# Two transformer blocks on one core: the order of the PSUM banks in the down products, other banks for one rotary slab, and a norm taken in two halves of the tokens

## The chip, the core and the metric

The kernel runs on one core of a Trainium2 chip. The metric is the device time of one execution in microseconds; times of a kernel are given as the median of several runs. One more execution, taken by the hardware profiler, is the one whose rows are shown here. TensorE (PE) multiplies and writes to PSUM, which has eight banks of 128 x 512 float32; VectorE (DVE), ScalarE (ACT) and SyncE's DMA queue do the rest. The granted clock is the clock of TensorE that the profile records, 1.0 for 2.4 GHz and 0.5 for 1.2 GHz.

## The reference

Two different blocks run one after the other over x of 512 tokens by 1024 features, all in float32. The first has attention (4 heads) beside a gated linear recurrence, a gated MLP with 2816 hidden features and a gated projection of a second input. The second has retention and a spatial gating branch, a normed output projection, and an MLP with a convolution over the tokens:

```
h = rms_norm(x, g_ffn); x = x + (silu(h @ w_gate) * (h @ w_up)) @ w_down          # first block
q, k, v, g, u, sv, a_ret, a_sgu = split(rms_norm(x, g_pre_mix_2) @ w_in_2)          # second block
merged = sigmoid(a_ret) * retention(rotary(q), rotary(k), v, g) + sigmoid(a_sgu) * sgu(u, sv)
x = x + rms_norm(merged @ w_out_2, g_post_mix_2)
h2 = rms_norm(x, g_pre_ffn_2)
x = x + rms_norm(conv_gated_mlp(h2, w_up_2, conv_w_2, conv_b_2, w_down_2), g_post_ffn_2)
```

## The kernel before

**Slabs.** The weights come as 130 slabs of at most 128 x 2048, in the order of the list `slabs`, through a ring of three buffers. SyncE loads a slab as soon as TensorE has finished the one three before it. For each slab ScalarE writes `slab_hi`, a float32r copy (L1873, `split`), and VectorE writes `slab_lo`, the rest (L1067, `split`). Activations are split in the same way into `h_hi` and `h_lo`. A product is then three matmuls, hi by hi, hi by lo and lo by hi (`three`, L380 to L382), and so nearly all matmuls of the kernel carry these three lines.

**Order.** Each engine's program is a Python function (`tensor_program`, `vector_program`, `scalar_program`, `sync_program`), written out by hand in the order in which the engine runs it. Engines wait for each other by semaphores. TensorE's results go into the eight PSUM banks: `take(name, b)` makes TensorE wait until the reader of what bank b held before is done, and `whole` tells the readers that a tile is complete. `slab_fm` multiplies one slab of 256 output features into two tiles of 128 features by 512 tokens; without another choice slab g takes the banks 2*(g%2) and 2*(g%2)+1. `rot` hands out the banks 4 to 7 in turn for small tiles.

**The down products of the first block** (`down`). Eight tiles of 128 features by 512 tokens, one in each bank, are summed over 11 slabs. All eight banks are taken ahead of the first matmul. The slab before (the last `up` slab) has its tiles in banks 0 and 1; VectorE reads them at L1490.

**The second block's down products** (`down_tokens`) are the same with the tokens on the partitions: block t of 128 tokens has its two halves of the features in banks 2t and 2t+1. All eight banks are again taken first. The last `b2up` tiles are in banks 0 and 1, read at L1109.

**The rotary slabs.** The second block starts with four slabs for queries and keys. Slabs IN2 and IN2+1 run together and fill four tiles in banks 2, 3, 0, 1; slabs IN2+2 and IN2+3 take banks 2, 3 and 0, 1 again. Of each tile ScalarE copies the two halves (L2210, L2211) and VectorE multiplies the tile itself out of its bank (L1567).

**The norm behind w_out.** Four slabs give eight tiles `o2`. ScalarE squares each (L2329, into `tmp[k]`) and copies it with its gain (L2330), VectorE sums the squares into `tmp[0]` (L1080), TensorE sums over the features with matmuls of one column (L441), ScalarE takes the root (L1878), VectorE the reciprocal (L1091) and lays it on a diagonal (L1094, `diagonal`), and TensorE multiplies ones by it (L990), which gives the row `post_row` of 512 tokens on all partitions. For each tile k VectorE multiplies `o2` by the row (L1785) and adds it to the residual `xT` (L1790); ScalarE writes `h_hi` (L2347) and a square for the next norm (L2348), and VectorE `h_lo` (L1072). Then the first two `up` slabs of the convolution MLP, UP2 and UP2+1, run together, tile k of the features after tile k, over four banks. Behind them VectorE sums the squares and splits slab UP2+2.

**The attention part.** In the loop over n (8 passes) ScalarE copies the transposed softmax weights of unit u out of PSUM (`transposed`, L2007), which TensorE's value products wait for (L694), and from n = 5 on rounds a gated head to `gated_hi` (`head_output`, L2063), which VectorE needs for `gated_lo`. From n = 6 on `transposed` has nothing left to do there.

## Time and profile before

| | us |
|---|---|
| median of 3 runs | 1635.32 |
| lowest, highest | 1631.61, 1635.99 |
| the profiled execution, its whole time | 1637.03 |
| its span | 1635.7 |
| TensorE busy in it | 1610.8 |
| VectorE, ScalarE busy in it | 885.4, 650.7 |
| mean granted clock | 0.994 |

The span is the time from the first to the last record of the profiled execution. TensorE's matmuls overlap: a matmul of 512 columns is recorded as 0.39 us long while the next one starts 0.23 us after it. In the chain of waits each piece therefore counts from one end to the next. The granted clock is 1.0 for the whole span except for three stretches, near 82 to 93 us, near 1257 to 1267 us and at the very end.

### The profile page before, as it was taken

Reading aid. Unit: us, or ns where it says so; the run is one execution under the profiler, and the core shown is the slowest. Engines: PE = TensorE matmul, PEld = TensorE weight load, DVE = VectorE, ACT = ScalarE, POOL = GpSimd, SP = SyncE. Lnnn points to the kernel's source line nnn. Section 1 sums busy time; section 2 is a strip of 40 time slices with the busy share of each in tenths; the row PEclk is TensorE's granted clock in tenths of the full one; section 3 lists DMA queues with packets and bytes.
Section 4 is the critical chain, followed back from the end, with each engine's and each line's share of the span. In section 5 each row is a group of like instructions: output and inputs, shape, how many; then the busy total and the mean of one; then the engine's idle time right before and its main releaser. Section 6 shows DMA issues by size and latency. Waiting matters only on the chain.

```text
span 1635.7 us, 17948 instructions
## 1 busy us (share of the span) xinstructions
PE 1610.8 (98%) x7508; PEld 1318.6 (81%) x7508; DVE 885.4 (54%) x1178; ACT 650.7 (40%) x783; POOL 11.7 (1%) x25
## 2 busy tenths in 40 slices
PE   7999999999999999999999999999998999999998
PEld 6787777888888888888798888888886888888887
DVE  5646656774444441257655644354444787766313
ACT  4536657543232221155443433223334453444212
POOL 1000000000000000000000000000000000000000
PEclk9989999999999999999999999999998999999999
DMA  5311110213333323323221133222323232232232
GB/s 166 97 52 58 46 52 27 71 59 116 103 103 103 96 86 103 103 97 103 89 99 52 56 105 103 82 89 88 103 77 103 78 104 82 99 103 92 101 103 78
DMA packets 117216, 144.25 MB, mean 88 GB/s; under 512 B 6017, under 2 KB 103648, under 8 KB 117136
## 3 DMA queue, kind: packets, MB, share of 16 engines
q1 hardware_dynamic: 115712, 139.88, 26.1%
q0 software_dynamic: 1232, 3.16, 0.6%
q8 instruction: 60, 0.98, 0.3%
q14 instruction: 20, 0.16, 0.0%
q10 hardware_dynamic: 192, 0.07, 0.0%
HBM read 140.99 MB, written 2.10 MB: 87 GB/s over the span
## 4 chain that ended last, share of the span: by engine, by line
PE 95%; ACT 2%; DVE 2%; DMA 1%; issue 0%; SPq 0%; POOL 0%; DVEq 0%; ACTq 0%
PE bank L380 28%; PE bank L382 28%; PE bank L381 28%; PE bank L913 1%; PE bank L676 1%; PE bank L694 1%; PE bank L675 1%; PE bank L739 1%; PE bank L896 1%; PE bank L615 1%; PE bank L441 1%; ACT slab_hi L1873 1%; PE bank L734 1%; DMA slab_raw<-in_w_in 0%; PE bank L685 0%
## 5 line engine op out<-in xcount | busy, mean ns | idle before, releaser
L380 PE MATMUL bank<-h_hi,slab_hi 128*128 128x512 f32 x1192 | 473.9, 398 | 5.2 <-DVE h_lo L1072 3.1
L1067 DVE TENSOR_TENSOR slab_lo<-slab_raw,slab_hi 128x2048 fp32r<-128x2048 f32 x130 | 296.1, 2278 | 334.3 <-ACT slab_hi L1873 333.7
L382 PE MATMUL bank<-h_hi,slab_lo 128*128 128x512 f32 x1192 | 466.1, 391 | 0.0
L381 PE MATMUL bank<-h_lo,slab_hi 128*128 128x512 f32 x1192 | 465.8, 391 | 0.0
L1873 ACT ACTIVATE slab_hi<-slab_raw 128x2048 fp32r<-128x2048 f32 x130 | 246.5, 1897 | 175.1 <-DMA slab_raw<-in_w_down 142.6
L380 PEld LDWEIGHTS bank<-h_hi,slab_hi 128*128 128x128 f32 x1192 | 224.8, 189 | 58.4 <-issue 10.3
L381 PEld LDWEIGHTS bank<-h_lo,slab_hi 128*128 128x128 f32 x1192 | 225.0, 189 | 47.9 <-issue 2.2
L382 PEld LDWEIGHTS bank<-h_hi,slab_lo 128*128 128x128 f32 x1192 | 224.8, 189 | 47.5
L1109 DVE TENSOR_TENSOR tmp<-bank,x_rstd_rows 128x512 f32<-128x512 f32 x98 | 66.6, 687 | 95.7 <-PE bank L382 95.6
L380 PE MATMUL bank<-slab_hi,h_hi 128*128 128x256 f32 (+1 forms) x224 | 74.8, 334 | 0.0
L382 PE MATMUL bank<-slab_hi,h_lo 128*128 128x256 f32 (+1 forms) x224 | 73.6, 328 | 0.0
L381 PE MATMUL bank<-slab_lo,h_hi 128*128 128x256 f32 (+1 forms) x224 | 73.5, 328 | 0.0
L380 PE MATMUL bank<-slab_hi,hid_hi 128*128 128x512 f32 x176 | 68.6, 389 | 0.8 <-issue 0.8
L380 PE MATMUL bank<-hid_hi,slab_hi 128*128 128x512 f32 x176 | 68.5, 389 | 0.8 <-issue 0.8
L381 PE MATMUL bank<-slab_lo,hid_hi 128*128 128x512 f32 x176 | 68.5, 389 | 0.0
L382 PE MATMUL bank<-hid_hi,slab_lo 128*128 128x512 f32 x176 | 68.5, 389 | 0.0
L381 PE MATMUL bank<-hid_lo,slab_hi 128*128 128x512 f32 x176 | 68.5, 389 | 0.0
L382 PE MATMUL bank<-slab_hi,hid_lo 128*128 128x512 f32 x176 | 68.5, 389 | 0.0
L2366 ACT ACTIVATE tmp<-tmp,param_cols 128x512 f32<-128x512 f32 x44 | 35.2, 814 | 76.8 <-DVE tmp L1109 76.7
L380 PE MATMUL bank<-y_hi,slab_hi 128*128 128x512 f32 x128 | 50.3, 393 | 0.0
L382 PE MATMUL bank<-y_hi,slab_lo 128*128 128x512 f32 x128 | 49.8, 389 | 0.0
L381 PE MATMUL bank<-y_lo,slab_hi 128*128 128x512 f32 x128 | 49.8, 389 | 0.0
(417 smaller groups left out, 2142.7 us busy)
## 6 DMA issues: line engine op xcount, KB each, us to landing
slab_raw<-in_w_in SPq DMA_DIRECT2D x40, 1024.0 KB, 5.0
slab_raw<-in_w_up SPq DMA_DIRECT2D x33, 1024.0 KB, 5.0
slab_raw<-in_w_down SPq DMA_DIRECT2D x22, 1024.0 KB, 4.9
slab_raw<-in_w_gate SPq DMA_DIRECT2D x11, 1024.0 KB, 5.2
slab_raw<-in_w_o SPq DMA_DIRECT2D x4, 1024.0 KB, 4.9
slab_raw<-in_w_ple_gate SPq DMA_DIRECT2D x4, 1024.0 KB, 5.0
slab_raw<-in_w_ret_o SPq DMA_DIRECT2D x4, 1024.0 KB, 4.9
slab_raw<-in_w_sgu_o SPq DMA_DIRECT2D x4, 1024.0 KB, 4.9
```

Of the source, the lines that this page charges most:

```text
L380: T.matmul(ps, a_hi, b_hi, start=start, stop=False, skip_group_check=skip)
L381: T.matmul(ps, a_hi, b_lo, start=False, stop=False, skip_group_check=skip)
L382: return T.matmul(ps, a_lo, b_hi, start=False, stop=stop, skip_group_check=skip)
L441: ins = T.matmul(dst[:, t:t + 1], sq[:, chunk[t]], ones[:, 0:1], start=clear and t == 0, stop=last, skip_group_check=True)
L615: ins = T.matmul(sums[:, c:c + which.shape[1]], tmp[n % 4][:, chunk[t]], which, start=n == 0 and t == 0, stop=n >= 5, skip_group_check=True)
L675: T.matmul(ps[:, :], q_nope[:, hd, chunk[j]], k_nope[:, hd, :], start=True, stop=False)
L676: whole(("score", u), T.matmul(ps[:, :], q_rope[half, hd // 2, chunk[j]], k_rope[half, hd // 2, :], start=False, stop=True))
L694: ins = T.matmul(ps[:, :], v_mla[:, kb, hd * VH:(hd + 1) * VH], p_t[:, kb, :], start=kb == 0, stop=kb == TT - 1)
L1067: V.tensor_tensor(w_lo[j][:, 0:n], raw[j][:, 0:n], w_hi[j][:, 0:n].bitcast(F32), ALU.subtract).then_inc(slab_lo, 1)
L1109: V.tensor_tensor(dst, t.ps[:, :], xrow[:, :], ALU.mult).then_inc(t.free, 1)
L1873: A.activation(w_hi[j][:, 0:n], raw[j][:, 0:n], ACT.Copy).then_inc(slab_hi, 1)
L2366: A.activation(acc[t], hid[t], ACT.Identity, scale=col("conv_w1", f[t]), bias=col("conv_b_2", f[t])).then_inc(conv_mid, 1)
```

## The change

**The down products.** `down` takes each bank only when its first product is due, in slab 0, and goes through slab 0 in another order of the banks: 4, 5, 6, 7, then the two that the slab before last had, then the two of the last slab. `down_tokens` does the same by blocks of tokens: 2, 3, 1, 0. The other slabs keep their order.

**The rotary slab.** IN2+2 takes banks 4 and 5. IN2+3 keeps 0 and 1.

**The norm behind w_out.** VectorE's last addition of squares is left out; TensorE sums tile 0 (the sum of seven) and tile 7 into the same column of a bank. The diagonal, the row product (banks 7 and 5), and for tile 0 the product, the addition and `h_hi` go by halves of 256 tokens. In the first two `up` slabs TensorE takes, for each k, the products of `h_hi` first (eight matmuls, for k = 0 sixteen of half the width) and waits for `h_lo` only then (four matmuls). For the tiles behind tile 0 VectorE's product is also two instructions, one from each bank.

**ScalarE's order.** `head_output` stands behind `transposed`.

```diff
-        def slab_fm(g, names, src_hi=h_hi, src_lo=h_lo, ready=None, src=None):
+        def slab_fm(g, names, src_hi=h_hi, src_lo=h_lo, ready=None, src=None, b=None):
...
-            ps = [take(names[t], 2 * (g % 2) + t) for t in range(2)]
+            ps = [take(names[t], (2 * (g % 2) if b is None else b) + t) for t in range(2)]
...
         def down(g0, name, hi, lo, lo_done):
-            ps = [take((name, n), n) for n in range(KT)]
+            last = 2 * ((g0 - 1) % 2)
+            order = [4, 5, 6, 7, 2 - last, 3 - last, last, last + 1]
...
-                for n in range(KT):
+                for n in order if s == 0 else range(KT):
+                    ps = tile[name, n].ps if s else take((name, n), n)
...
-        for n in range(2, 4):
-            slab_fm(IN2 + n, [("rot", 2 * n), ("rot", 2 * n + 1)])
+        slab_fm(IN2 + 2, [("rot", 4), ("rot", 5)], b=4)
+        slab_fm(IN2 + 3, [("rot", 6), ("rot", 7)])
...
-        whole("post_sum", sum_rows(ps[:, 0:TT], tmp[0], True, True))
-        T.wait_ge(post_diag, 1)
-        ps = take("post_row", 7, post_done, KT)
-        whole("post_row", T.matmul(ps[:, :], ones, tmp[1], start=True, stop=True))
+        sum_rows(ps[:, 0:TT], tmp[0], False, True)
+        T.wait_ge(post_squared, KT)
+        whole("post_sum", sum_rows(ps[:, 0:TT], tmp[KT - 1], True, False))
+        for half in range(2):
+            T.wait_ge(post_diag, half + 1)
+            ps = take(("post_row", half), 7 - 2 * half, post_done, KT)
+            whole(("post_row", half), T.matmul(ps[:, 0:CW], ones, tmp[1][:, half * CW:(half + 1) * CW], start=True, stop=True))
...
         for k in range(KT):
-            for s in range(2):
-                part(wv, s, names, *h_k, k, k + 1, h_ready(5))
+            for half in range(2 if k == 0 else 1):
+                tok = slice(half * CW, (half + 1) * CW) if k == 0 else slice(0, S)
+                if k == 0 and half == 0:
+                    T.wait_ge(first_hi_half, 1)
+                else:
+                    T.wait_ge(h_hi_done, 8 * 5 + k + 1)
+                for n in range(4):
+                    hv, lv = wv[n // 2]
+                    cols_t, ps = slice((n % 2) * P, (n % 2 + 1) * P), tile[names[n]].ps
+                    T.matmul(ps[:, tok], hv[:, k, cols_t], h_hi[:, k, tok], start=k == 0 and half == 0, stop=False,
+                             skip_group_check=True)
+                    T.matmul(ps[:, tok], lv[:, k, cols_t], h_hi[:, k, tok], start=False, stop=False, skip_group_check=True)
+            T.wait_ge(h_lo_done, 8 * 5 + k + 1)
+            for n in range(4):
+                hv, cols_t = wv[n // 2][0], slice((n % 2) * P, (n % 2 + 1) * P)
+                ins = T.matmul(tile[names[n]].ps[:, :], hv[:, k, cols_t], h_lo[:, k, :], start=False, stop=k == KT - 1,
+                               skip_group_check=True)
...
-        ps = [take(("down2", n), n) for n in range(2 * TT)]
+        last = (DOWN2 - 1) % 2
+        blocks_first = [2, 3, 1 - last, last]
...
+                ps = take(("down2", 2 * t + half), 2 * t + half) if f == 0 else tile["down2", 2 * t + half].ps
...
-            for t in range(TT):
+            for t in range(TT) if s else blocks_first:
```

On VectorE and ScalarE:

```diff
-        sum_tiles(tmp, post_squared, 0, 5, KT - 1)
+        sum_tiles(tmp, post_squared, 0, 5, KT - 1, post_summed)
         split(UP2 + 1)
-        sum_tiles(tmp, post_squared, 0, KT - 1, KT, post_summed)
         rstd(rcol[:, 0:TT], "post_sum")
-        diagonal(tmp[1], rcol[:, 0:TT], post_diag)
...
+        for half in range(2):
+            t, tok = tile["post_row", half], slice(half * CW, (half + 1) * CW)
+            V.wait_ge(psum_ready, t.done)
+            V.wait_ge(vector_step, step(V.tensor_tensor(tmp[2][:, tok], o2[:, 0, tok], t.ps[:, 0:CW], ALU.mult)))
+            V.tensor_tensor(xT[:, 0, tok], xT[:, 0, tok], tmp[2][:, tok], ALU.add).then_inc((post_half, post_done)[half], 1)
...
+        A.wait_ge(post_half, 1)
+        A.activation(h_hi[:, 0, 0:CW], xT[:, 0, 0:CW], ACT.Identity, scale=col("g_pre_ffn_2", 0)).then_inc(first_hi_half, 1)
         for k in range(KT):
             A.wait_ge(post_done, k + 1)
-            A.activation(h_hi[:, k, :], xT[:, k, :], ACT.Identity, scale=col("g_pre_ffn_2", k)).then_inc(h_hi_done, 1)
+            tok = slice(0 if k else CW, S)
+            A.activation(h_hi[:, k, tok], xT[:, k, tok], ACT.Identity, scale=col("g_pre_ffn_2", k)).then_inc(h_hi_done, 1)
```

TensorE at the start of the first down products, before. The last row of the `up` slab (source `h_hi`) stands first; the names behind the arrow are what streams and what is loaded as weights, with the number of the buffer.

```order
L382 MATMUL bank1<-h_hi_66,slab_lo1_61 128x512
L380 MATMUL bank0<-hid_hi_117,slab_hi2_65 128x512
L381 MATMUL bank0<-hid_lo_118,slab_hi2_65 128x512
L382 MATMUL bank0<-hid_hi_117,slab_lo2_62 128x512
L380 MATMUL bank0<-hid_hi_117,slab_hi2_65 128x512
```

And now (line numbers here and below are those of the changed kernel):

```order
L383 MATMUL bank1<-h_hi_66,slab_lo1_61 128x512
L381 MATMUL bank4<-hid_hi_117,slab_hi2_65 128x512
L382 MATMUL bank4<-hid_lo_118,slab_hi2_65 128x512
L383 MATMUL bank4<-hid_hi_117,slab_lo2_62 128x512
L381 MATMUL bank4<-hid_hi_117,slab_hi2_65 128x512
```

The product behind the last `up` tile (bank 1) goes to bank 4 instead of bank 0, and bank 1 comes last, 42 matmuls later.

TensorE at the norm behind w_out, before: the last product of w_out, the sum over features, the row, and the first products of UP2 and UP2+1.

```order
L382 MATMUL bank1<-merged_hi_144,slab_lo0_60 128x512
L441 MATMUL bank6<-const_small_sb_77,tmp0_69 128x1 x4
L990 MATMUL bank7<-tmp1_70,const_small_sb_77 128x512
L380 MATMUL bank2<-h_hi_66,slab_hi1_64 128x512
L381 MATMUL bank2<-h_lo_67,slab_hi1_64 128x512
L382 MATMUL bank2<-h_hi_66,slab_lo1_61 128x512
```

And now:

```order
L383 MATMUL bank1<-merged_hi_144,slab_lo0_60 128x512
L442 MATMUL bank6<-const_small_sb_77,tmp0_69 128x1 x4
L442 MATMUL bank6<-const_small_sb_77,tmp7_76 128x1 x4
L997 MATMUL bank7<-tmp1_70,const_small_sb_77 128x256
L997 MATMUL bank5<-tmp1_70,const_small_sb_77 128x256
L1019 MATMUL bank2<-h_hi_66,slab_hi1_64 128x256
L1021 MATMUL bank2<-h_hi_66,slab_lo1_61 128x256
```

There are two sums and two half rows, and the first product of `h_lo` has moved from the second to the seventeenth matmul of the slab pair.

VectorE at the same place, before:

```order
L1080 TENSOR_TENSOR tmp_69<-tmp_69,tmp_76 128x512
L1091 RECIPROCAL rstd_cols<-rstd_cols 128x4
L1094 TENSOR_TENSOR tmp_70<-const_small_sb,rstd_cols 128x512
L1785 TENSOR_TENSOR tmp_71<-mixed_out,bank 128x512
L1790 TENSOR_TENSOR residual<-residual,tmp_71 128x512
L1785 TENSOR_TENSOR tmp_72<-mixed_out,bank 128x512
L1072 SCALAR_TENSOR_TENSOR h_lo<-residual,param_cols,h_hi 128x512
L1790 TENSOR_TENSOR residual<-residual,tmp_72 128x512
```

And now:

```order
L1118 RECIPROCAL rstd_cols<-rstd_cols 128x4
L1804 TENSOR_TENSOR tmp_70<-const_small_sb,rstd_cols 128x256 x2
L1811 TENSOR_TENSOR tmp_71<-mixed_out,bank 128x256
L1812 TENSOR_TENSOR residual<-residual,tmp_71 128x256
L1811 TENSOR_TENSOR tmp_71<-mixed_out,bank 128x256
L1812 TENSOR_TENSOR residual<-residual,tmp_71 128x256
L1821 TENSOR_TENSOR tmp_72<-mixed_out,bank 128x256 x2
L1099 SCALAR_TENSOR_TENSOR h_lo<-residual,param_cols,h_hi 128x512
L1827 TENSOR_TENSOR residual<-residual,tmp_72 128x512
```

The addition of squares (L1080) is gone, the diagonal and the work on tile 0 stand in halves, and two halves stand for each later product.

## Rows read from the trace of the kernel before

**Rows 1.** The page: busy us of each engine, share of the span, instructions.

```profile
PE 1610.8 (98%) x7508; PEld 1318.6 (81%) x7508; DVE 885.4 (54%) x1178; ACT 650.7 (40%) x783; POOL 11.7 (1%) x25
```

**Rows 2.** The chain of waits at the first down products: start us, us, what.

```profile
591.60 0.83 issue
592.43 0.47 PE bank L380
592.90 0.23 PE bank L381
```

**Rows 3.** The timeline of VectorE there: start us, us, engine, line, operation, [idle before].

```profile
591.64 0.69 DVE L1490 TENSOR_TENSOR tmp<-tmp,bank 128x512 f32<-128x512 f32 x1 [2.60 <-PE bank L382]
```

**Rows 4.** The timeline of TensorE at the second block's down products.

```profile
1510.66 0.47 PE L380 MATMUL bank<-slab_hi,hid_hi 128*128 128x512 f32 x1 [0.83 <-issue]
```

**Rows 5.** The chain of waits ahead of the third rotary slab.

```profile
792.26 0.61 DVE ret_qk L1567
...
793.01 0.47 PE bank L380
```

**Rows 6.** The timeline of TensorE ahead of the third rotary slab.

```profile
791.87 0.39 PE L382 MATMUL bank<-h_hi,slab_lo 128*128 128x512 f32 x1
```

**Rows 7.** The chain of waits in the attention part.

```profile
281.85 0.52 ACT gated_hi L2063
282.37 0.49 ACT weights_t L2007
282.90 3.70 PE bank L694 x8
```

**Rows 8.** The chain of waits at the norm behind w_out.

```profile
1253.33 0.61 ACT tmp L2329
...
1253.96 0.70 DVE tmp L1080
...
1254.71 1.07 PE bank L441 x8
...
1256.31 0.70 DVE tmp L1094
...
1257.05 2.09 PE bank L990 x2
...
1259.16 0.70 DVE tmp L1785
...
1260.61 0.73 ACT h_hi L2347
...
1261.37 0.76 DVE h_lo L1072
...
1262.27 0.76 PE bank L380
```

**Rows 9.** Groups by line: engine, operation, xcount | busy us, mean ns | idle.

```profile
L1626 DVE COPY ret_state_b<-bank 128x256 f32<-128x256 f32 x4 | 1.7, 424 | 0.1
...
L1897 ACT ACTIVATE ret_v<-bank,x_rstd_cols 128x256 f32<-128x256 f32 x4 | 1.9, 474 | 17.7 <-PE bank L382 17.7
```

**Rows 10.** The timeline of TensorE among products of 256 columns.

```profile
843.01 0.28 PE L380 MATMUL bank<-slab_hi,h_hi 128*128 128x256 f32 x1
843.13 0.28 PE L381 MATMUL bank<-slab_lo,h_hi 128*128 128x256 f32 x1
```

**Rows 11.** The timeline of VectorE, slab UP2+2.

```profile
1282.01 2.29 DVE L1067 TENSOR_TENSOR slab_lo<-slab_raw,slab_hi 128x2048 fp32r<-128x2048 f32 x1
```

**Rows 12.** The timeline of TensorE, its first matmul on slab UP2+2.

```profile
1287.12 0.49 PE L380 MATMUL bank<-h_hi,slab_hi 128*128 128x512 f32 x1
```

**Rows 13.** Stretches: us, busy time by engine, PEclk (granted clock), DMA share, GB/s.

```profile
1256.00:1257.00 1.00, 0.00 (x0) 0.00 (x0) 0.87 (x2) 0.06 (x1) 0.00 (x0) 0.82 1.08 385
...
1266.00:1267.00 1.00, 1.00 (x5) 0.77 (x3) 1.00 (x3) 0.14 (x1) 0.00 (x0) 0.56 0.00 0
```

**Rows 14.** A stretch in the first block's query projection, same columns.

```profile
82.50:83.50 1.00, 1.00 (x4) 0.81 (x3) 0.00 (x0) 0.00 (x0) 0.00 (x0) 0.50 0.00 0
```

More of the change, by code:

```diff
@@ L1769, in vector_program @@
         split(UP2)
[L1770 removed]
+        sum_tiles(tmp, post_squared, 0, 5, KT - 1, post_summed)
         split(UP2 + 1)
[L1774 removed]
         rstd(rcol[:, 0:TT], "post_sum")
[L1776 to L1779 removed]
+        for half in range(2):
+            two = slice(2 * half, 2 * half + 2)
+            V.tensor_tensor(per_tile(tmp[1])[:, two, :], ident.unsqueeze(1).broadcast_to([P, 2, P]),
+                            rcol[:, two].unsqueeze(2).broadcast_to([P, 2, P]), ALU.mult).then_inc(post_diag, 1)
+        emptied(("o2", 0))
+        for half in range(2):
+            t, tok = tile["post_row", half], slice(half * CW, (half + 1) * CW)
+            V.wait_ge(psum_ready, t.done)
+            V.wait_ge(vector_step, step(V.tensor_tensor(tmp[2][:, tok], o2[:, 0, tok], t.ps[:, 0:CW], ALU.mult)))
+            V.tensor_tensor(xT[:, 0, tok], xT[:, 0, tok], tmp[2][:, tok], ALU.add).then_inc((post_half, post_done)[half], 1)
+        for k in range(1, KT + 1):
             if k < KT:
@@ L1784, in vector_program @@
                 emptied(("o2", k))
-                scaled_step = step(V.tensor_tensor(w, o2[:, k, :], t.ps[:, :], ALU.mult))
-            if k:
-                norm_tile(5, k - 1, "g_pre_ffn_2")
+                for half in range(2):
+                    tok = slice(half * CW, (half + 1) * CW)
+                    scaled_step = step(V.tensor_tensor(w[:, tok], o2[:, k, tok], tile["post_row", half].ps[:, 0:CW], ALU.mult))
+            if k == 1:
+                V.wait_ge(first_hi_half, 1)
+            norm_tile(5, k - 1, "g_pre_ffn_2")
             if k < KT:
@@ L2104, in scalar_program @@
             transposed(unit)
+            if n >= 5:
+                head_output(n - 5)
             unit += 1
```

12 lines of the change are left out of this document (5 added, 7 removed).

## The prediction, made before the changed kernel was run

> **What bounds the kernel now.** I read the page's busy times first, then the chain of waits, then the timeline at the places that the diff touches. TensorE is busy for 98% of the span [rows 1], so an edit can only pay where TensorE stands still or runs at the lower clock, and any VectorE or ScalarE time elsewhere is free as long as it stays hidden. The steady spacing of two 512-column matmuls is 0.23 us [rows 2]. Against that spacing the chain shows five holes at edited places: one ahead of the first block's down products, one ahead of the third rotary slab, one inside the attention part, one ahead of the second block's down products, and a large one at the norm behind w_out.
>
> **The banks of the down products.** Before the first matmul all eight banks are asked for. The last one to come free is that of the last `up` tile, which VectorE reads from 591.64 for 0.69 us [rows 3]. TensorE's hole is 0.83 us, and the first matmul behind it takes 0.47 us where 0.23 is the rule [rows 2], so 0.83 + 0.24 = 1.07 us. After the change bank 4 is asked for alone, and the late bank stands last of eight: seven banks at six matmuls of 0.23 us is 9.6 us of cover, against 0.7 us of need. The hole goes, **-1.07 us**. Nothing else takes its place: the slab and the `hid_lo` tiles of slab 0 were made long before. The second down products show the same 0.83 and 0.47 us [rows 4]; the last `b2up` tiles stand in banks 0 and 1, and token block 0 now goes last in slab 0, again with over 8 us of cover: **-1.07 us**.
>
> **The rotary slab.** Its tiles 4 and 5 take banks 2 and 3 from tiles 0 and 1. VectorE's read of tile 1 ends at 792.87 and TensorE starts at 793.01 [rows 5]; its last matmul had begun at 791.87 [rows 6], so the steady start would be 792.10. The second matmul of the restart ends 1.0 us later than in a steady stream (793.48 is the end of the first, 792.49 would be): **-1.0 us**. Banks 4 and 5 were last used for the norm's sum and row, read by then. What is late next? Tiles 6 and 7 stay in banks 0 and 1, where tiles 2 and 3 are read several us before; the value tiles that want banks 4 and 5 come a whole slab later, 48 matmuls or 10.9 us.
>
> **ScalarE's order in the attention part.** For n = 5 alone both operations exist. The copy `weights_t` starts at 282.37, right behind `gated_hi` with its 0.52 us, and TensorE starts at 282.90 when it is whole [rows 7]. With the copy first it is whole 0.52 us earlier: **-0.5 us**. `gated_hi` and its reader on VectorE come 0.5 us later; the states that TensorE needs next are then due some 2 us before their use.
>
> **The norm behind w_out.** The old path runs from 1253.33 to 1262.27, 8.9 us [rows 8]. The new one, step by step:
> 1. Square of tile 7, 0.63 as before.
> 2. VectorE's last addition, 0.70 us, is gone from the path. Instead TensorE sums two tiles. The first sum needs nothing late and runs beside the square; one group costs 1.07 us [rows 8], so it ends near 1254.1 to 1254.3, and the second at about 1255.1, where the old one ended at 1255.78. Gain about 0.7 (0.5 if the groups don't overlap at all).
> 3. Root and reciprocal, 0.53 us, unchanged.
> 4. Half a diagonal. No 128x256 TENSOR_TENSOR stands in the trace; a COPY of that size takes 0.42 us, a scaled copy on ScalarE 0.47 [rows 9], against 0.70 for the whole. I take 0.42 + 0.04.
> 5. Half the row product: 1.04 of 2.09 us, as before at the lower clock.
> 6. Half a product and half an addition on VectorE, 0.44 each for 0.72 each.
> 7. `h_hi` by half, 0.49 for 0.75.
> 8. `h_lo`, 0.76 us, is no longer waited for, since the first eight matmuls read h_hi alone. The 0.14 us to issue stay.
> The sum is 1.77 + 0.53 + 0.46 + 1.06 + 0.88 + 0.49 + 0.14 = 5.3 us, so TensorE starts near 1258.65: **-3.6 us**. Then 16 matmuls of 256 columns stand for 8 of 512; their spacing is 0.12 us [rows 10], so +0.1 us. The second half of h_hi is due 0.9 us behind the first, h_lo 0.9 us after that; eight matmuls of 256 columns take 1.0 us at the full clock and 1.7 at half, so TensorE hardly waits.
>
> What is late next is VectorE. It splits slab UP2+2 behind the norm: that ends at 1284.30 [rows 11], and TensorE wants it at 1287.12 [rows 12], 2.8 us of slack. TensorE comes 3.6 us earlier. VectorE's products begin 2.0 us earlier, but it pays 0.3 us more for tile 0 and up to 0.15 us (0.42 twice for 0.70) for each of seven others. So the split ends 0.6 to 1.7 us earlier, at 1282.6 to 1283.7, and is wanted at 1283.5: between 0.9 us of slack and 0.2 us of wait. I take no wait.
>
> **The clock.** It fell at about 1256.6 (0.82 over that microsecond) and rose at 1266.9 (0.56) [rows 13], so TensorE ran its first 4.6 us of matmuls at 1.2 GHz, which costs 2.3 us. The new path still leaves TensorE with little to do for over 3 us (two groups of one-column sums, then a pause, then a short product, then a pause), so I take the same loss again, with 0.8 us either way for where the rise falls. The row at 82.5 us, at 0.50 [rows 14], shows that short pauses among thin matmuls can lower it too.
>
> **The sum.** 1.07 + 1.07 + 1.0 + 0.5 + 3.6 - 0.1 = 7.2 us. The profiled execution took 1637.03 us (span 1635.7 and 1.3 around it), which gives 1629.8. The median of the runs shown lies 0.1% below it, at 1635.32; the same ratio gives **1628.1 us**, 0.44% faster.
>
> **Rivals.**
> A, the forecast: 1628.1, by itself 1626.5 to 1630. Chance 0.62.
> B, the clock stays up or rises early at the norm. The pauses are now 1 to 1.5 us each, where the longest was 3.1. That gives back up to 2.3 us and 0.5 us of the row product: 1625.3. For it: shorter pauses. Against: [rows 14]. Chance 0.12. The Trainium skill ("TensorE: Matmul & The Clock Gate", HAM oscillation) blames long idle gaps alone; by that B would be the likelier, and the trace at 82.5 us speaks against it.
> C, the norm gives half. VectorE's halves cost nearly a whole operation each, 0.6 for 0.70: four steps on the path then save 0.1 instead of 0.26, so the path is 0.6 us longer, tile 0 costs VectorE 1.0 us more than before and each of the seven later pairs some 0.5. The split of slab UP2+2 then ends at 1284.3 - 1.4 + 1.0 + 3.5 = 1287.4 and is wanted at 1284.1. That gives back 0.6 + 3.3 = 3.9 us: 1632.0. The point from which it decides is 0.45 us for a half. Against it are the sizes in [rows 9]. Chance 0.16. The Trainium skill ("VectorE: DVE Perf Modes", the TRN2 errata) advises tiles of 512 elements or more because each instruction pays a fixed part; by that rule the halves are a mistake, and here what counts is the time to the first half, not VectorE's total.
> D, the edits at the down products do nothing, because the bank that is asked for first is also late. Against: banks 4 to 7 hold transposes read long before. Both terms fall out: 1630.2. Chance 0.06.
> E, slower. In the first slab of both down products eight waits now stand one by one between matmuls. If each, though satisfied, stops the preloading of weights, 14 added stops are paid. A stop with a real wait costs 1.0 us [rows 5, 6]; at that price the kernel is 14 - 7.2 = 7 us slower, 1642. It decides from 0.51 us a stop. Against: slabs begin all over the trace with three waits and no hole. Chance 0.04.
>
> **Numbers.** The bound of 0.3% (4.9 us, about what a measurement of this kernel can tell from no change) lies at 1630.4. Most of C, half of D and a twentieth of A lie above it. So faster 0.76, same 0.20, slower 0.04. The range reaches from B less the clock's 0.8 us to C, and the runs before span 4 us by themselves: 1624.5 to 1632.5.
>
> **What would show it.** In the profile after: no hole ahead of either down product, nor ahead of the third rotary slab; `weights_t` ahead of `gated_hi`; TensorE's first h_hi matmul 5.3 us behind the square of tile 7, the diagonal halves at 0.42 us; a low stretch of 4 to 5 us behind it; no idle TensorE ahead of slab UP2+2. A hole of 1 us or more there, or waits between the banks of slab 0, would make the prediction wrong.

## The result and the profile after

| | before | after |
|---|---|---|
| median, us | 1635.13 (4 runs) | 1625.53 (4 runs, 1624.66 to 1628.76) |
| ratio | | 0.995, interval 0.9935 to 0.9965 |
| the profiled execution | 1637.03 | 1628.76 |
| its span | 1635.7 | 1627.5 |
| TensorE busy | 1610.8 | 1608.6 |

The forecast was 1628.1 us within 1624.5 to 1632.5. The medians differ by 9.6 us where 7.2 were predicted; the profiled executions differ by 8.2 us of span. Ratios leave out slow executions: one of the kernel before, drawn beside `late_sum`, `best_a` and `best_b` below, took 5535 us.

The page of the changed kernel gives the busy time of each engine, as in [rows 1]. Line numbers are from here on those of the kernel that is spoken of; in the changed one `three` is L381 to L383.

```profile
PE 1608.6 (99%) x7526; PEld 1319.1 (81%) x7526; DVE 885.4 (54%) x1187; ACT 651.0 (40%) x784; POOL 11.7 (1%) x25
```

But for 18 matmuls more at the norm, both traces run the same ones in nearly the same order. So one can take the start of a matmul before, less its start after, and see where this difference, called the offset from here on, grows. That is the whole account of the 8.2 us:

| place | a matmul before, after | gained there |
|---|---|---|
| up to 100 us, code that the change doesn't touch | 100.19, 98.62 | 1.57 |
| ScalarE's order, attention part | 282.90, 280.80 | 0.53 |
| first down products | 593.66, 590.46 | 1.10 |
| third rotary slab | 794.02, 789.79 | 1.03 |
| norm behind w_out | 1286.31, 1278.48 | 3.60 |
| second down products, their start | 1512.13, 1503.19 | 1.11 |
| second down products, second slab | 1521.87, 1513.60 | -0.67 |

The changed places give 6.7 us. Of the 1.57 us in the first row, 0.14 stand already at 60 us and 1.43 arise in the query projection near 82 us, where nothing was changed.

**First down products.** TensorE's timeline, against [rows 2]: start us, us, engine, line, operation. The first product of `hid_hi` follows 0.23 us behind the last `up` matmul.

```profile
589.10 0.39 PE L383 MATMUL bank<-h_hi,slab_lo 128*128 128x512 f32 x1
589.33 0.39 PE L381 MATMUL bank<-hid_hi,slab_hi 128*128 128x512 f32 x1
```

VectorE's read of the last `up` tile, against [rows 3], now lies beside TensorE's products, and its bank is wanted 9.6 us later:

```profile
589.53 0.69 DVE L1517 TENSOR_TENSOR tmp<-tmp,bank 128x512 f32<-128x512 f32 x1 [2.60 <-PE bank L383]
```

**Third rotary slab**, TensorE's timeline, against [rows 5, 6]: no hole.

```profile
788.66 0.39 PE L383 MATMUL bank<-h_hi,slab_lo 128*128 128x512 f32 x1
788.89 0.39 PE L381 MATMUL bank<-h_hi,slab_hi 128*128 128x512 f32 x1
```

**Attention part**, ScalarE's timeline, against [rows 7]: the copy that TensorE wants now stands first.

```profile
280.17 0.58 ACT L2044 ACTIVATE weights_t<-bank 128x512 f32<-128x512 f32 x1
280.65 0.62 ACT L2100 ACTIVATE gated_hi<-z 128x512 fp32r<-128x512 f32 x1
```

**The norm behind w_out**, the chain of waits (start us, us, what), against [rows 8]. The x16 row is both sums over features; from it to the last row is the new path.

```profile
1249.05 1.75 PE bank L442 x16
...
1250.83 0.27 ACT rstd_cols L1915
...
1251.34 0.44 DVE tmp L1804
...
1251.82 0.71 PE bank L997 x2
...
1252.62 0.43 DVE tmp L1811
...
1253.08 0.44 DVE residual L1812
...
1253.54 0.52 ACT h_hi L2383
1254.06 0.14 issue
1254.19 0.55 PE bank L1019
```

**Second down products.** TensorE no longer stands ahead of their first slab, but ahead of their second. Its timeline there, with the idle time and its releaser in brackets:

```profile
1512.49 0.39 PE L383 MATMUL bank<-slab_hi,hid_lo 128*128 128x512 f32 x1
1513.26 0.50 PE L381 MATMUL bank<-slab_hi,hid_hi 128*128 128x512 f32 x1 [0.39 <-DVE slab_lo L1094]
1513.60 0.39 PE L382 MATMUL bank<-slab_lo,hid_hi 128*128 128x512 f32 x1
```

What it waits for, on ScalarE and VectorE:

```profile
1507.58 1.28 ACT L2415 ACT_TABLE_LOAD   x1
1508.87 0.20 ACT L2415 ACTIVATE rstd_cols<-const_small_sb 128x1 f32<-128x1 f32 x1
1508.98 3.70 ACT L1910 ACTIVATE slab_hi<-slab_raw 128x2048 fp32r<-128x2048 f32 x2
```

```profile
1510.91 4.50 DVE L1094 TENSOR_TENSOR slab_lo<-slab_raw,slab_hi 128x2048 fp32r<-128x2048 f32 x2 [2.63 <-ACT slab_hi L1910]
```

ScalarE finishes `hid_hi` of the last tiles, loads its table for the square root (1.28 us) and only then splits the next slab; VectorE's first `slab_lo` of the pair is whole 2.3 us later, at 1513.2, where steady products would want it at 1512.7. In the kernel before, the same piece stood here, VectorE's timeline and then TensorE's:

```profile
1518.75 4.49 DVE L1067 TENSOR_TENSOR slab_lo<-slab_raw,slab_hi 128x2048 fp32r<-128x2048 f32 x2 [2.63 <-ACT slab_hi L1873]
```

```profile
1521.65 0.39 PE L380 MATMUL bank<-slab_hi,hid_hi 128*128 128x512 f32 x1
```

It was whole at 1521.0 and wanted at 1521.65: 0.6 us of slack. Taking 1.07 us away upstream spent it. The Trainium skill ("ScalarE: Activation LUTs", What ACT_TABLE_LOAD costs) gives 1.28 us for the load and some 1.38 us of drain beside it. The trace agrees on the load; the next operation starts 0.01 us behind it and the load itself 0.02 us behind `hid_hi`, so no such drain shows here.

**Slab UP2+2**, VectorE's split and TensorE's first matmul on it, against [rows 11, 12]:

```profile
1275.60 2.28 DVE L1094 TENSOR_TENSOR slab_lo<-slab_raw,slab_hi 128x2048 fp32r<-128x2048 f32 x1
```

```profile
1279.29 0.49 PE L381 MATMUL bank<-h_hi,slab_hi 128*128 128x512 f32 x1
```

Whole at 1277.9, used at 1279.3: 1.4 us of slack are left of 2.8, and no wait.

**The clock.** Stretches of 12 us over the two places where it falls: us, busy time by engine, granted clock, DMA share, GB/s. One less the granted clock, times 24, is the length of the stretch at 1.2 GHz. Before:

```profile
82.00:94.00 12.00, 12.00 (x45) 10.37 (x44) 2.61 (x5) 2.06 (x4) 0.00 (x0) 0.57 0.01 1
1256.00:1268.00 12.00, 7.81 (x18) 5.08 (x19) 8.90 (x15) 4.75 (x9) 0.00 (x0) 0.57 0.15 52
```

After:

```profile
82.00:94.00 12.00, 12.00 (x57) 10.41 (x56) 2.96 (x5) 3.63 (x4) 0.00 (x0) 0.73 0.09 17
1252.00:1264.00 12.00, 11.12 (x45) 9.20 (x45) 10.89 (x24) 6.50 (x11) 0.00 (x0) 0.72 0.12 42
```

At 82 us it is 10.2 us at the lower clock before and 6.8 us after (the latter began at 81.7). At the norm it is 10.2 and 6.8 us too, but of these only what has matmuls in it costs: 4.6 us before, 5.1 us after (1254.19 to 1259.3). The norm's gain is thus 3.84 us at the first product and 3.60 us at the end. The fall comes 3.5 us behind the last product of w_out in both traces; what differs is how long the clock stays low.

### The profile page after: what moved, and what is told of

Read it like the earlier page. It is cut to its first block, busy times and chain, and to the rows that moved or that the text cites. A ratio compares the mean times of both kernels' runs of the same rounds, so it can differ in the third digit from the quotient of the medians.

```text
span 1627.5 us, 17987 instructions
## 1 busy us (share of the span) xinstructions
PE 1608.6 (99%) x7526; PEld 1319.1 (81%) x7526; DVE 885.4 (54%) x1187; ACT 651.0 (40%) x784; POOL 11.7 (1%) x25
## 4 chain that ended last, share of the span: by engine, by line
PE 95%; DVE 2%; ACT 1%; DMA 1%; issue 0%; SPq 0%; POOL 0%; DVEq 0%; ACTq 0%
PE bank L381 28%; PE bank L383 28%; PE bank L382 28%; PE bank L917 1%; PE bank L677 1%; PE bank L695 1%; PE bank L676 1%; PE bank L740 1%; PE bank L900 1%; PE bank L442 1%; ACT slab_hi L1910 1%; DVE slab_lo L1094 1%; PE bank L616 1%; DMA slab_raw<-in_w_in 1%; PE bank L1019 1%; PE bank L735 1%
## 5 line engine op out<-in xcount | busy, mean ns | idle before, releaser
L381 PE MATMUL bank<-h_hi,slab_hi 128*128 128x512 f32 x1160 | 460.1, 397 | 1.6 <-DVE h_lo L1156 1.3
L383 PE MATMUL bank<-h_hi,slab_lo 128*128 128x512 f32 x1160 | 452.7, 390 | 0.0
L382 PE MATMUL bank<-h_lo,slab_hi 128*128 128x512 f32 x1160 | 452.2, 390 | 0.0
L381 PEld LDWEIGHTS bank<-h_hi,slab_hi 128*128 128x128 f32 x1160 | 218.3, 188 | 51.2 <-issue 4.4
L382 PEld LDWEIGHTS bank<-h_lo,slab_hi 128*128 128x128 f32 x1160 | 218.3, 188 | 46.7 <-issue 2.2
L383 PEld LDWEIGHTS bank<-h_hi,slab_lo 128*128 128x128 f32 x1160 | 218.1, 188 | 46.1
L381 PE MATMUL bank<-slab_hi,h_hi 128*128 128x256 f32 (+1 forms) x224 | 74.8, 334 | 0.0
L383 PE MATMUL bank<-slab_hi,h_lo 128*128 128x256 f32 (+1 forms) x224 | 73.6, 328 | 0.0
L381 PE MATMUL bank<-slab_hi,hid_hi 128*128 128x512 f32 x176 | 68.6, 390 | 0.4 <-DVE slab_lo L1094 0.4
L383 PE MATMUL bank<-slab_hi,hid_lo 128*128 128x512 f32 x176 | 68.5, 389 | 0.0
L381 PE MATMUL bank<-hid_hi,slab_hi 128*128 128x512 f32 x176 | 68.5, 389 | 0.0
L383 PE MATMUL bank<-hid_hi,slab_lo 128*128 128x512 f32 x176 | 68.5, 389 | 0.0
L381 PE MATMUL bank<-y_hi,slab_hi 128*128 128x512 f32 x128 | 50.3, 393 | 0.0
L383 PE MATMUL bank<-y_hi,slab_lo 128*128 128x512 f32 x128 | 49.8, 389 | 0.0
```

Of the source, the lines that this page charges most:

```text
L381: T.matmul(ps, a_hi, b_hi, start=start, stop=False, skip_group_check=skip)
L382: T.matmul(ps, a_hi, b_lo, start=False, stop=False, skip_group_check=skip)
L383: return T.matmul(ps, a_lo, b_hi, start=False, stop=stop, skip_group_check=skip)
```

## Experiments

Each kernel was also run with a profile, and its matmuls set against those of the kernel before, or of the changed one, as in the table above. At most places that tells a few hundredths of a microsecond, where the medians tell one or two microseconds of the whole. At the norm it tells less: three traces with the same code there gained 3.47, 3.60 and 3.84 us, because the clock fell at different moments.

### The parts of the change apart: norm_alone and rest_alone

`norm_alone` is the kernel before with the diff's part on the norm; `rest_alone` is the kernel before with all the others. No line is in both.

> The kernel before with the norm part of the change alone (two sums on TensorE, halves for the diagonal, the row and tile 0, products of h_hi first). Theory A (each part of the change is worth what the offset between the two traces shows at its place): 3.6 us faster than the kernel before, ratio 0.9978; TensorE's first h_hi matmul 5.1 us behind the start of the square of tile 7; the holes of 0.83 us ahead of both down products and of 0.76 us ahead of the third rotary slab are still there. Rival B (the measured 9.6 us are all due to the change, so the parts are worth more than their places show): norm and the rest together give 9.6, so this one some 5 us, ratio 0.997. Rival C (the norm's gain is given back at slab UP2+2): under 1 us faster. Of the early low clock stretch near 82 us A expects either of the two lengths seen (10.2 or 6.8 us), without a link to the change.

Measured: 1631.03 us (12 runs) against 1634.2 us (35 runs of the kernel before), ratio 0.9981, interval 0.9969 to 0.9994. The offset grows by 3.47 us at the norm (from 4.92 to 8.39) and by no more than 0.1 us elsewhere behind 100 us.

> The kernel before with all but the norm part: bank orders of both down products, banks 4 and 5 for the third rotary slab, ScalarE's order in the attention part. Theory A: 0.53 + 1.10 + 1.03 + 0.44 = 3.1 us faster, ratio 0.9981: in its trace the matmuls run 0.5 us earlier behind 283 us, 1.1 more behind 592, 1.0 more behind 793, and at the second down products 1.1 us more at first and 0.67 less from slab DOWN2+1 on, where TensorE waits for VectorE's split. Rival B: about 4.6 us or more, ratio 0.997. Rival D (per-bank waits cost something): less than 2 us.

Measured: 1630.68 us (11 runs), ratio 0.9982, interval 0.9971 to 0.9993. The offset grows by 0.50, 1.11 and 1.02 us at the three places, by 1.10 at the start of the second down products, and falls by 0.66 at their second slab: 3.1 us. At the norm, whose code is that of the kernel before here, it falls by 0.13.

The two ratios make 0.9963 together, 6.0 us, where the places make 6.5: theory A holds. By itself the interval of `norm_alone` still takes in its rival's 0.997, and that of `rest_alone` only just leaves it out; `after_again` decides against 9.6 us.

The early stretch shows the same freedom. In the trace of `norm_alone`, whose code up to there is that of the kernel before, the clock does not fall near 82 us at all:

```profile
82.00:94.00 12.00, 12.00 (x75) 10.50 (x73) 6.24 (x8) 4.06 (x5) 0.00 (x0) 1.00 0.29 89
```

Against the profiled execution before (10.2 us at the lower clock) its matmuls gain 4.8 us between 82 and 93 us, of which 4.6 are left at 100 us.

### The changed kernel once more: after_again

> The changed kernel itself, in many more runs than the four behind its result. Theory A (the change is worth 3.1 + 3.6 = 6.7 us, as its places in the trace and the two partial kernels show, and the rest of the 9.6 us is the scatter of both kernels' runs): about 6.7 us faster than before, ratio 0.9959, with single runs at distances that fit other lengths of the stretch at the lower clock near 82 us. Rival B (something off these places pays 3 us more): ratio 0.9941 or lower.

Measured: 1629.81 us (6 runs, 1625.39 to 1630.6) against 1635.41, ratio 0.9962, interval 0.9949 to 0.9975. Its profiled execution has 10.2 us at the lower clock at 82 us, as that of the kernel before:

```profile
82.00:94.00 12.00, 12.00 (x46) 10.26 (x45) 2.63 (x5) 2.08 (x4) 0.00 (x0) 0.57 0.01 1
```

and its span is 1628.8: with equal stretches there the spans differ by 6.9 us. Rival B (0.9941 or lower) lies outside the interval. The change is worth 6.7 to 6.9 us; the other 3 of the 9.6 are which runs were drawn. The mean granted clock that is recorded for every run bears this out. Of the ten runs of the changed kernel, the four with a mean of 0.996 or more took 1624.7 to 1626.0 us, the six with 0.995 took 1626.7 to 1630.6; three of the former were among the first four. Of 68 runs of the kernel before, the 35 with 0.994 or less have a median of 1636.2 us, the 33 with 0.995 or more one of 1631.8.

At the norm this trace gains 3.84 us, not 3.60. The chain of waits has, against the 0.71 us at 1251.82 above:

```profile
1253.39 1.23 PE bank L997 x2
...
1256.29 0.55 PE bank L1019
```

The clock fell at 1253.0, ahead of the row product instead of amid it. So TensorE's first product came 0.5 us later, 5.67 us behind the start of the sums, but only 3.5 us of the low stretch, instead of 5.1, had such products in them.

### What the halves bring: whole_tile0

```diff
-        for half in range(2):
-            T.wait_ge(post_diag, half + 1)
-            ps = take(("post_row", half), 7 - 2 * half, post_done, KT)
-            whole(("post_row", half), T.matmul(ps[:, 0:CW], ones, tmp[1][:, half * CW:(half + 1) * CW], start=True, stop=True))
+        T.wait_ge(post_diag, 1)
+        ps = take("post_row", 7, post_done, KT)
+        whole("post_row", T.matmul(ps[:, :], ones, tmp[1], start=True, stop=True))
```

and on VectorE and ScalarE the loops of the kernel before.

> The changed kernel with the halves undone: the diagonal, the row product and tile 0's product, addition and h_hi are whole again, later products too; the two sums on TensorE and the order with the products of h_hi first stay. By the prediction's steps (0.26 for the diagonal, 0.3 to 1.0 for the row product, 0.56 for product and addition, 0.26 for h_hi, less 0.1 for sixteen half matmuls) it is 1.3 to 2.0 us slower than the changed kernel, so 4.7 to 5.4 us faster than before by the offsets, and TensorE's first h_hi matmul stands 6.5 to 7.1 us behind the square of tile 7 (5.1 in the changed kernel). Rival (halves are worth nothing, since VectorE loses with them what the path gains; order and sums bring it all): same time as the changed kernel.

Measured: 1629.36 us (12 runs), ratio 0.9975, interval 0.9963 to 0.9987. The chain of waits at its norm:

```profile
1245.68 1.75 PE bank L441 x16
...
1247.96 0.70 DVE tmp L1116
...
1248.71 2.09 PE bank L995 x2
...
1252.27 0.73 ACT h_hi L2368
...
1253.13 0.77 PE bank L1014
```

From the sums' start to the first product it takes 7.45 us, where the changed kernel takes 5.14. The norm gains 1.14 us instead of 3.60, so the kernel with halves is 2.46 us ahead, a little over the expected 1.3 to 2.0 (2.70 against `after_again`). Two matters of the clock are in that number. The row product takes 2.09 us whole and its first half 0.71, because the clock fell at 1248.4 here, ahead of it, and at 1252.4 in the changed kernel, amid it. And it stayed low for 10.2 us here, for 6.8 us there. Had it stayed low for 10.2 us in the changed kernel too, 8.5 us of its matmuls would have run at 1.2 GHz instead of 5.1, which would cost 1.7 us more (an estimate from these stretches). All seven traces in which the clock fell at a norm with halves have 6.8 us there, the three with whole tiles 10.2 us. So the shorter stretch may be the halves' own doing; nothing here separates it from them. Two sums and the order with h_hi first bring the 1.14.

### What the order with h_hi first brings: lo_awaited

```diff
                 if k == 0 and half == 0:
-                    T.wait_ge(first_hi_half, 1)
+                    T.wait_ge(h_lo_done, 8 * 5 + 1)
```

> The changed kernel with one wait more: ahead of the first product of h_hi in slab UP2 TensorE waits for h_lo of tile 0 too, as the kernel before did. The order of the matmuls is as in the changed kernel. If taking the products of h_hi first is what pays, TensorE starts behind VectorE's h_lo, at 1255.7 instead of 1254.2 on the changed kernel's clock: 1.5 us later, and later h_hi tiles are then ready earlier than needed, so all of 1.5 us stays: 1.5 us slower than the changed kernel. Rival (TensorE catches up, because it waits for h_lo of tile 0 or for h_hi of tile 1 anyway a little later): 0 to 0.5 us slower.

Measured: 1628.0 us (12 runs), ratio 0.9973, interval 0.9959 to 0.9986. The chain of waits:

```profile
1247.17 1.75 PE bank L442 x16
...
1253.06 0.76 DVE h_lo L1099
...
1253.95 0.55 PE bank L1019
```

The path is 6.78 us, 1.64 longer, as the theory has it. The norm's gain shrinks by 0.91 us only, 3.60 to 2.69. The low stretch is again 6.8 us long and ends at 1257.6, so that only 3.6 us of it have products of `h_hi` or `h_lo` in them instead of 5.1: waiting longer at the lower clock gives some 0.7 us back. Neither theory had this; the delay inside the low stretch cost about half of itself.

### Do satisfied waits cost anything: more_waits

```diff
                     ps = tile[name, n].ps if s else take((name, n), n)
+                    T.wait_ge(slab_lo, g + 1)
```

and the same ahead of each bank of the second down products.

> The changed kernel with a wait that is long satisfied (for the slab in use) ahead of each bank's product in the down products, about 150 waits more. Theory (a satisfied wait between matmuls costs nothing): spacing of 0.227 us on both sides of each, same span. Rival E of the prediction (each stops the preloading of weights, 0.51 us or more): 77 us slower; at a hundredth of that price still 1.5 us.

Measured: 152 waits more, one execution; span 1629.1 against 1628.8 of `after_again`, whose low stretches are as long, and the 0.3 us stand already at 60 us. TensorE's timeline over the first of these waits:

```profile
590.85 0.39 PE L383 MATMUL bank<-h_hi,slab_lo 128*128 128x512 f32 x1
591.08 0.39 PE L381 MATMUL bank<-hid_hi,slab_hi 128*128 128x512 f32 x1
```

A satisfied wait costs nothing that the trace resolves. Rival E is out.

### The new wait at the second down products: split_early

```diff
+            if n == FT // 2 - 1:
+                split(DOWN2 + 1)
             for t in range(2):
                 A.wait_ge(conv_gated, 2 * n + t + 1)
...
         A.activation(rcol[:, 0:1], eps_col, ACT.Sqrt)
-        for s in range(FT // 2 - 1):
+        for s in range(1, FT // 2 - 1):
```

> The changed kernel; ScalarE splits the second slab of the second down products (DOWN2+1) ahead of the last hid_hi instead of behind the load of its table for the square root. Theory (the wait of 0.66 us that took the place of the removed one at the second down products is VectorE's split of this slab, which hangs on ScalarE's, 1.28 us of table load and the two hid_hi behind each other): slab_hi of it is whole at 1505.5 instead of 1510.9 on the changed kernel's clock, VectorE's part at 1510.6 instead of 1513.2, TensorE wants it at 1512.7, no wait: 0.66 us faster than the changed kernel, and the matmuls of the second down products keep their 0.23 us throughout. Rival 1 (ScalarE is late with hid_hi by the 1.9 us, and TensorE waits for the last two hid tiles or for slab DOWN2+2): no gain. Against it: ScalarE stands idle for 2.7 us just there.

Measured: 1625.63 us (6 runs), ratio 0.9946, interval 0.9933 to 0.9958. ScalarE's split, and TensorE over the border of the two slabs:

```profile
1504.12 1.90 ACT L1910 ACTIVATE slab_hi<-slab_raw 128x2048 fp32r<-128x2048 f32 x1
```

```profile
1513.12 0.39 PE L383 MATMUL bank<-slab_hi,hid_lo 128*128 128x512 f32 x1
1513.35 0.39 PE L381 MATMUL bank<-slab_hi,hid_hi 128*128 128x512 f32 x1
```

0.23 us, no wait: the offset to the changed kernel grows by 0.66 us just here. So the split behind the table load was the new bound. The ratio moves by more than that, which only says how far a ratio scatters.

### The clock at the norm: warm_norm

```diff
+        T.wait_ge(held[4].free, held[4].value)
+        T.wait_ge(slab_lo, UP2 + 1)
...
+        for _ in range(4):
+            T.matmul(bank[4][:, :], w_hi[(UP2) % RING][:, 0:P], w_hi[(UP2) % RING][:, 0:S], start=True, stop=True, skip_group_check=True)
         for half in range(2):
             T.wait_ge(post_diag, half + 1)
```

and six more behind the rows. The two waits stand ahead of the sums.

> The changed kernel with ten matmuls added whose result nobody reads (512 columns, slab UP2 by itself, into the free bank 4): four ahead of the wait for the diagonal, six behind the row product. They fill TensorE's pauses at the norm (1.03 and 0.88 us and the time between). Theory (the clock falls because TensorE does little at the norm, and that costs half of the 5.1 us of matmuls behind it): the clock stays at 1.0 there and the kernel is 2.5 us faster than the changed kernel. Rival 1 (the clock falls all the same, at 1252.4 or earlier, since the sums of one column stay): then the added matmuls take 0.43 us each, the last ones end behind h_hi, and the kernel is 0 to 1.5 us slower. Rival 2 (the clock has nothing to do with these pauses): same low stretch at the same place, same time.

Measured: 1625.43 us (5 runs), ratio 0.9936, interval 0.9923 to 0.9949. The clock stays up:

```profile
1252.00:1264.00 12.00, 12.00 (x61) 9.69 (x62) 10.33 (x23) 5.54 (x10) 0.00 (x0) 1.00 0.24 85
```

The offset to the changed kernel grows by 2.22 us at the norm, where 2.5 were forecast from the matmuls at half clock, and then falls by 0.9 at slab UP2+2 (1.4 us are left behind it), VectorE's timeline and TensorE's:

```profile
1277.12 2.29 DVE L1100 TENSOR_TENSOR slab_lo<-slab_raw,slab_hi 128x2048 fp32r<-128x2048 f32 x1
```

```profile
1279.46 0.50 PE L381 MATMUL bank<-h_hi,slab_hi 128*128 128x512 f32 x1 [0.73 <-DVE slab_lo L1100]
```

This is the wait that the prediction weighed for the change itself. The 1.4 us of slack were less than the 2.2 gained, with the restart behind it. The Trainium skill ("TensorE: Matmul & The Clock Gate", HAM oscillation) blames idle gaps of TensorE, long ones, for such falls. On the gaps the traces agree: with the sums of one column unchanged and only the waits filled, the clock did not fall at the norm in any of the four kernels that have the added matmuls; without them it fell in all ten. On the length they do not: the longest gap of the changed kernel there is 1.03 us.

### The early stretch: late_sum

```diff
             whole(("q", t), ins)
-            if t:
-                sum_squares(t - 1)
+            for n in ((), (0,), (), (1, 2), (3,), (4,))[t]:
+                sum_squares(n)
```

> The changed kernel; in the first block's query projection the sum of squares of tile 1 goes behind tile 3's products instead of tile 2's. Theory (the early stretch at the lower clock, 0, 6.8 or 10.2 us long in the traces so far, follows from the wait of 0.92 us and the sums of one column at 79 to 82 us, and it is what most of the scatter of a kernel's runs consists of): the wait of 0.92 us goes with its 0.24 us behind it, 1.2 us faster than the changed kernel in every run; if the clock now stays up there, another 1.7 to 3.4 us (the matmuls between the sums take twice their time for 6.8 or 10.2 us less what they wait in any case), so 1.2 to 4.5 us in all, and the runs scatter less than the 4 to 5 us of the changed kernel. Rival (the thin activity, not the wait, lowers the clock; the sums are as thin as before): 1.2 us alone, and the scatter stays.

Measured: 1624.76 us (6 runs, 1623.03 to 1625.23), ratio 0.9943, interval 0.9928 to 0.9957. TensorE's timeline in the changed kernel:

```profile
80.61 1.05 PE L616 MATMUL bank<-const_small_sb,tmp 128*128 128x1 f32 x8 [0.92 <-ACT tmp L2002]
```

And now, a tile later; the bracket is what is left of the wait:

```profile
79.24 0.40 PE L383 MATMUL bank<-cq_hi,slab_lo 128*128 128x512 f32 x1
79.89 0.50 PE L381 MATMUL bank<-cq_hi,slab_hi 128*128 128x512 f32 x1 [0.26 <-DVE q_nope L1141]
```

and the clock there:

```profile
82.00:94.00 12.00, 12.00 (x75) 10.37 (x75) 6.17 (x9) 4.56 (x6) 0.00 (x0) 1.00 0.28 89
```

Its trace ends 3.5 us ahead of the changed kernel's, whose stretch was 6.8 us, and its runs lie within 2.2 us where those of `after_again` lie within 5.2. In the three traces with this edit the clock never fell there; in the other eleven it fell nine times. So it is the wait rather than the number of the sums that lets it fall; that two sums now stand together is a change too, which this run does not separate. The runs of the eight kernels here that have the wait, and five runs or more, scatter over 4.6 to 6.9 us each, those of the three kernels without it over 2.2 to 3.2. What is left is not this clock: all five runs of `best_c` below have a mean of 1.000 and still lie 3.2 us apart.

### Adding up: best_a, best_b, best_c

`best_a` has the edits of `split_early` and `warm_norm`, and a new order around slab UP2+2: VectorE splits it amid the squares, and TensorE takes the sum over features two tiles later.

> The changed kernel with the early split of slab DOWN2+1, the ten added matmuls at the norm, and a mend for what those turned up: with the clock up TensorE waits 0.73 us (0.9 with the restart) for VectorE's split of slab UP2+2, so VectorE now splits it behind the fourth of eight tiles' squares, and TensorE takes two tiles' products of UP2+2 ahead of the sum over features and two more ahead of the row. Theory (gains add up by places): 0.66 + 2.25 = 2.9 us faster than the changed kernel, ratio to before about 0.994 (0.9959 less 0.18%). Rival (VectorE is the bound behind the norm in total, so the wait moves to the sum, the row or slab UP2+3): 2.0 us or less, with a wait of TensorE of 0.7 us or more between 1280 and 1292.

Measured: 1626.76 us (9 runs), ratio 0.9967, interval 0.9953 to 0.998. This was a miss. TensorE's timeline, two slabs on, and VectorE's copy of the norm's row:

```profile
1301.99 0.50 PE L381 MATMUL bank<-h_hi,slab_hi 128*128 128x512 f32 x1 [1.22 <-DVE slab_lo L1101]
```

```profile
1283.68 0.69 DVE L1136 COPY x_rstd_rows<-bank 128x512 f32<-128x512 f32 x1 [2.55 <-PE bank L454]
```

TensorE waits 1.22 and, at 1336, 0.83 us for VectorE's splits. In `warm_norm` the row is copied at 1282.03, after 1.81 us of idleness; counted from the last product of w_out, which comes 1.56 us later in that trace, this is 3.2 us sooner. The wait at UP2+2 went, and at 1292 us 1.9 of the 2.2 us gained at the norm are still there. But VectorE stood idle for 2.55 us ahead of a row that TensorE now made late, and by 1336 us the offset had fallen by 2.6. In all its trace ends 0.1 us ahead of the changed kernel's. The rival holds (2.0 us or less); the waits came later than the 1280 to 1292 us where it had put them.

`best_b` adds the edit of `late_sum`.

> As best_a, with the later sum in the query projection (late_sum) too. Theory: best_a's 2.9 us and late_sum's 1.2 to 4.5 us add up: 4.1 to 7.4 us faster than the changed kernel, ratio to before 0.991 to 0.9935, the fastest of all kernels here. Rival (if late_sum gains nothing beyond its wait): 1.2 us better than best_a at most.

Measured: 1624.72 us (6 runs), ratio 0.9942, interval 0.9927 to 0.9958: the gain of `late_sum` alone and not the 4.1 to 7.4 us expected, since the same loss stands in its trace: 2.6 us between 1292 and 1336.

`best_c` is `best_b` with the old order around slab UP2+2.

> The changed kernel with the early split of slab DOWN2+1, the ten added matmuls at the norm and the later sum in the query projection, but without best_a's other order around slab UP2+2. Theory (best_a lost at UP2+3 and the next slabs what the clock at the norm gave, because its row of the norm came 2 us later and VectorE, with little idle time there, never caught up; in the old order TensorE pays the wait of 0.9 us at UP2+2 and nothing behind it): late_sum's gain, 0.66 at the down products, and 2.25 less 0.9 at the norm: 2.0 us faster than late_sum, some 1622.8, ratio to before 0.993. Rival (any gain ahead of the convolution MLP is given back inside it): 0.7 us faster than late_sum at most, with waits of TensorE for VectorE's splits between 1290 and 1340.

Measured: 1622.91 us (5 runs, 1621.07 to 1624.23) against 1633.84, ratio 0.9938, interval 0.9925 to 0.9952; span 1619.8. The clock, over both places:

```profile
82.00:94.00 12.00, 12.00 (x73) 10.33 (x72) 6.45 (x8) 4.93 (x6) 0.00 (x0) 1.00 0.28 87
1248.00:1264.00 16.00, 16.00 (x79) 13.20 (x78) 14.78 (x30) 9.34 (x16) 0.00 (x0) 1.00 0.00 1
```

Against `late_sum` its trace gains 2.5 us at the norm, loses 0.8 at UP2+2 and gains 0.7 at the second down products, with no wait between 1290 and 1340: 2.4 us, where 2.0 were expected. It has the shortest span and the lowest median of all kernels here; 1.7 of the 4.1 us by which its span is shorter stand already at 60 us, in code that none of the edits touches. Its interval overlaps those of `warm_norm` and `late_sum`, so that it is the best of the three rests on the traces.

## Why the prediction was right, and where it was off

- **First down products, rotary slab, ScalarE's order.** Predicted 1.07, 1.0 and 0.5 us, measured 1.10, 1.03 and 0.53. A hole plus the slow first matmul behind it is what a restart costs. D is out.
- **Second down products.** Predicted 1.07, measured 0.44. The step that failed is the one that said that nothing else takes the hole's place. It asked for the banks only. The next slab's split had 0.6 us of slack in the trace of before, which the prediction never read there, though it did so at UP2+2.
- **The norm.** Predicted 3.6 at TensorE's first product less 0.1 behind it, 3.5; measured 3.84 less 0.24, 3.60 (3.47 in `norm_alone`, 3.84 in `after_again`). That forecast and first trace lie so close is luck in part: the two errors cancel. From the square to the first product: sums 1.77 against 1.74, root and reciprocal 0.53 and 0.51, diagonal 0.46 and 0.48, row 1.06 and 0.80, product and addition 0.88 and 0.92, `h_hi` 0.49 and 0.52, the issue the same. Only the row was mis-sized, because it began at the full clock; in `after_again`, where it did not, row and what follows up to VectorE take 1.33 us, more than predicted. TensorE so started 3.84 us sooner instead of 3.6, and paid 0.24 us behind that (products of half the width, and 0.5 us more of matmuls at the lower clock) where 0.1 was predicted.
- **Halves on VectorE** take 0.42 to 0.44 us, so C was out from its own threshold of 0.45. The Trainium skill ("VectorE: DVE Perf Modes", the TRN2 errata) advises against tiles under 512 elements. Here the kernel with them is 2.46 us ahead, the clock's part included, since VectorE's total was not what ended last; `warm_norm` shows where it would be, 1.4 us of slack away.
- **Slab UP2+2.** Predicted between 0.9 us of slack and 0.2 of wait, measured 1.4 of slack. A pair of halves takes VectorE 0.74 to 0.75 us in all, not the up to 0.84 that was allowed for.
- **The clock at the norm.** The same loss was predicted, with matmuls low for 4.6 us; it was 5.1. The prediction argued for the fall but not for where the rise comes, and that the loss came out is luck: the matmuls now begin 3.8 us sooner behind the fall, so with the stretch of before, 10.2 us, they would have run low for 8.5 us, and some 1.7 us of the gain (an estimate) would have gone. The stretch was 6.8 us long instead. B did not come true: the clock fell in all ten traces without filled waits.
- **What was in no term:** the stretch near 82 us. The prediction cited it as evidence on the norm and left out that its length is free between runs of the same code: 0, 6.8 or 10.2 us, worth up to 4.8 us. It moved the comparison of the two profiled executions by 1.4 us, and its like is the likeliest source of what the four medians show beyond 6.7. For runs without a profile there is only the mean granted clock, which goes with their times as told at `after_again` but does not say where the clock was low.
- **The sum** was added up as 7.2; its terms make 7.14.

## What to carry to other kernels

Where a hole on the bounding engine is removed, read the slack of every later input of that engine in the same stage, the next weights too; a gain larger than the smallest slack is cut to it. Halve the first tile behind a reduction when the path to the first product counts and the halving engine has slack. When two executions of nearly equal kernels are compared, set the starts of the same instructions against each other, place by place, before believing a difference of medians that is as large as the scatter. Where the clock falls near the place, read the length of the low stretch too, and in more than one trace.

## What the runs showed of the hardware

- TensorE's granted clock fell near 82 us after a single wait of 0.92 us among sums of one column, in nine of eleven traces, and stayed low for 6.8 or 10.2 us, differently for the same code. With the wait cut to 0.26 us there (three traces), or waits of 1 us filled at the norm (four traces), it stayed at 2.4 GHz at that place: 2.2 us gained at the norm, and without the early wait runs that scatter over 2.2 to 3.2 us instead of 4.6 to 6.9.
- A delay ahead of matmuls, inside a stretch at the lower clock that stays as long as it was, cost about half of itself (1.64 us of path, 0.91 us of time, one trace).
- 152 satisfied waits between matmuls cost nothing that a trace shows. A restart after a real one costs 0.1 us beyond the late start itself: the second matmul starts 0.34 us behind the first at 1513.26, where 0.23 is the rule.
